# Dense feed-forward: most pairs of gate and up as seven block products of half size, each third pair as before

## The reference

```python
def swiglu(h, w_gate, w_up, w_down):
    return (jax.nn.silu(h @ w_gate) * (h @ w_up)) @ w_down
# layer 0, D_MODEL = 1024, D_FF = 2816
h = rmsnorm(x, norm_ffn[layer])
x = x + swiglu(h, ffn_w_gate[j], ffn_w_up[j], ffn_w_down[j])
```

## Time and profile before

| | |
|---|---|
| three runs | 1555.54, 1556.11, 1556.99 us; median 1556.11 |
| profiled execution, its own time | 1556.81 us, span 1555.1 us |
| TensorE busy | 1538.5 us, 99% of the span |
| VectorE, ScalarE, GpSimd busy | 65%, 54%, 15% |
| mean granted clock of TensorE | 0.997 of full |

### The profile page before, as it was taken

The page is one execution under the profiler, slowest core; times in us unless marked ns, Lnnn a source line. Parts: engine busy times, 40 slices in busy tenths (PEclk is TensorE's granted clock), DMA queues, the critical chain, the costliest instruction groups (busy, mean ns, idle before and its releaser), DMA issues.

```text
span 1555.1 us, 23275 instructions
## 1 busy us (share of the span) xinstructions
PE 1538.5 (99%) x7960; PEld 1309.2 (84%) x7961; DVE 1009.2 (65%) x1689; ACT 834.3 (54%) x1330; POOL 236.7 (15%) x290
## 2 busy tenths in 40 slices
PE   9999999999999999999999999999999999999997
PEld 6888888888888888888888888879898888889895
DVE  7657765755444443336557765776676988887587
ACT  6436665433223322324447664475576888886564
POOL 0204564000000000002015662010000011110000
PEclk9999999999999999999999999999999999999998
...
GB/s 228 196 99 69 74 55 82 95 136 136 156 138 138 95 91 98 99 91 155 102 92 69 72 55 90 195 57 320 257 256 254 358 385 372 388 384 266 240 255 134
DMA packets 89787, 265.71 MB, mean 171 GB/s; under 512 B 12497, under 2 KB 22737, under 8 KB 89680
## 3 DMA queue, kind: packets, MB, share of 16 engines
...
...
## 4 chain that ended last, share of the span: by engine, by line
PE 96%; DVE 2%; DMA 1%; issue 1%; ACT 0%; SPq 0%; DVEq 0%; ACTq 0%; POOLq 0%
PE ps L1698 19%; PE ps L1703 19%; PE ps L1699 19%; PE ps L2052 8%; PE ps L2027 5%; PE ps L2029 5%; PE ps L2028 5%; PE ps L2054 3%; PE ps L1865 2%; PE ps L1898 1%; PE ps L2026 1%; PE ps L2025 1%; PE ps L1878 1%; PE ps L1897 1%; PE ps L1877 1%; PE ps L2013 1%
## 5 line engine op out<-in xcount | busy, mean ns | idle before, releaser
L808 ACT ACTIVATE w_hi<-raw 128x1024 fp32r<-128x1024 f32 (+1 forms) x168 | 176.0, 1047 | 337.1 <-PE ps L1703 333.8
L1698 PE MATMUL ps<-h_hi,w_hi 128*128 128x512 f32 x880 | 350.6, 398 | 0.6 <-DVE k_lo L1245 0.4
L1699 PE MATMUL ps<-h_lo,w_hi 128*128 128x512 f32 x880 | 343.6, 390 | 0.0
L1703 PE MATMUL ps<-h_hi,w_lo 128*128 128x512 f32 x880 | 343.4, 390 | 0.0
L1157 DVE TENSOR_TENSOR w_lo<-raw,w_hi 128x1024 fp32r<-128x1024 f32 x136 | 164.3, 1208 | 124.1 <-ACT w_hi L808 123.9
L1162 DVE TENSOR_TENSOR m_lo<-m_raw,m_hi 128x1024 fp32r<-128x1024 f32 x144 | 167.9, 1192 | 61.1 <-ACT m_hi L851 60.3
L1703 PEld LDWEIGHTS ps<-h_hi,w_lo 128*128 128x128 f32 x880 | 165.2, 188 | 35.4
L1698 PEld LDWEIGHTS ps<-h_hi,w_hi 128*128 128x128 f32 x880 | 165.6, 188 | 27.0 <-DVE k_lo L1245 0.8
L1699 PEld LDWEIGHTS ps<-h_lo,w_hi 128*128 128x128 f32 x880 | 166.0, 189 | 25.9 <-issue 0.7
L851 ACT ACTIVATE m_hi<-m_raw 128x1024 fp32r<-128x1024 f32 x144 | 145.4, 1031 | 53.0 <-PE ps L2026 25.9
L2052 PE MATMUL ps<-xt,m_hi 128*128 128x320 f32 x592 | 154.3, 347 | 0.3 <-issue 0.3
...
...
...
## 6 DMA issues: line engine op xcount, KB each, us to landing
...
```

The costliest lines, as they stand in the source:

```text
L808: A.activation(split_of(n, 0, cols)[0], raw[:, n % RAW, 0:cols], ACT.Copy).then_inc(hi_ready, 1)
L1698: E.matmul(ps[:, bank, :], wh, hi, start=first, stop=False)
L1699: E.matmul(ps[:, bank, :], wh, lo, start=False, stop=False)
L1703: return E.matmul(ps[:, bank, :], wl, hi, start=False, stop=final)
```

## The change

A gate tile and an up tile, each cut into two halves of the 1024 inputs, are a 2 by 2 block matrix; the input cut into two halves of features and two of tokens is another. Their product is eight block products, each of 4 tiles of inputs by 256 tokens, or seven, if sums and differences of blocks are multiplied (Winograd's form). Pairs 3, 4, 6, 7, 9, 10, 12, 13, 15, 16, 18 and 19 are now made with seven, the other ten (0, 1, 2, 5, 8, 11, 14, 17, 20, 21) with two units as before. A product is 12 matmuls of 256 columns.

The tables of the order are these. A job is a product (`seven`) or a unit; `w_hi` and `w_lo` are now four slots of half a unit, and `FREED_BY` tells which jobs can be split when job `x` is done. Of a pair's products 0, 4 and 5 take weights as they are, 1, 2, 3 and 6 take sums:

```diff
+SEVENS = [f for f in range(PLAIN, KF - 2) if (f - PLAIN) % 3 < 2]
+JOBS = [job for f in range(KF) for job in
+        ([("seven", f, j) for j in range(7)] if f in SEVENS else [("unit", f, j) for j in range(2)])]
...
+def frees(x):
+    last = SLOT[x] + (1 if JOBS[x][0] == "unit" else 0)
+    return max(y for y in range(x) if SLOT[y] <= last - 4)
+FREED_BY = {d: [x for x in range(2, len(JOBS)) if frees(x) == d] for d in range(len(JOBS))}
...
+def on_pool(x):
+    return JOBS[x][0] == "seven" and JOBS[x][2] == 5
...
+def seven_weights(f, j):
+    gate, up = FFN_START + 2 * f, FFN_START + 2 * f + 1
+    low, high = slice(0, T), slice(T, UNIT)
+    return ((gate, low), (None, 1), (None, 2), (None, 0), (gate, high), (up, high), (None, 2))[j]
```

A buffer of `raw` is refilled when all products of its pair have been split (SyncE):

```diff
-if n >= RAW:
-    sp.wait_ge(lo_ready, n - RAW + 1)
+m = n - RAW
+if FFN_START + 2 <= m < FFN_END:
+    f, j = (m - FFN_START) // 2, m % 2
+    if f in SEVENS:
+        sp.wait_ge(seven_lo, low_by(f))
+        sp.wait_ge(seven_lo_pool, SEVENS.index(f) + 1)
+    else:
+        sp.wait_ge(seven_lo, LOW_COUNT[JOB[("unit", f, j)]])
+elif n >= RAW:
+    sp.wait_ge(lo_ready, m + 1)
```

GpSimd forms the sums of weights, four for a pair, in three tiles (`norm`, `y_other`, `y_sum`), the low part of product 5, and two of the four sums of tokens:

```diff
+    pool.tensor_tensor(sums[0][:], up[:, 0:T], up[:, T:UNIT], ALU.add).then_inc(sums_ready, 1)
+    pool.wait_ge(sums_ready, 4 * q + 1)
+    pool.tensor_tensor(sums[1][:], sums[0][:], gate[:, 0:T], ALU.subtract).then_inc(sums_ready, 1)
...
+    pool.tensor_tensor(sums[2][:], gate[:, 0:T], up[:, 0:T], ALU.subtract).then_inc(sums_ready, 1)
+if part == 2:
+    pool.wait_ge(sums_ready, 4 * q + 2)
+    pool.wait_ge(seven_lo, split(q, 2))
+    pool.tensor_tensor(sums[2][:], gate[:, T:UNIT], sums[1][:], ALU.subtract).then_inc(sums_ready, 1)
...
+x = JOB[("seven", SEVENS[q], 5)]
+pool.wait_ge(seven_hi, x - 1)
+hi, lo = job_split(x)
+pool.tensor_tensor(lo, job_full(x), hi.bitcast(F32), ALU.subtract).then_inc(seven_lo_pool, 1)
...
+if layer == 0:
+    pool.wait_ge(h32_ready, KD)
+    pool.wait_ge(t_full_ready, 2)
+    pool.tensor_tensor(t_full(2), h_block(0, second_half), h_block(0, first_half), ALU.subtract).then_inc(t_full_ready, 1)
+    pool.tensor_tensor(t_full(3), h_block(1, first_half), t_full(0), ALU.subtract).then_inc(t_full_ready, 1)
+    for part in range(3):
+        weight_sums(0, part)
+    for q in range(1, len(SEVENS)):
+        if q % 2:
+            weight_sums(q, 0)
+            low_on_pool(q - 1)
+        else:
+            low_on_pool(q - 1)
+            weight_sums(q, 0)
+        weight_sums(q, 1)
+        weight_sums(q, 2)
+    low_on_pool(len(SEVENS) - 1)
```

ScalarE first writes the normalised input in full precision (`h_full`, 8 tiles), then follows the jobs. Behind the second of two such pairs it does both silus and both high parts:

```diff
-split_hi(FFN_START + 2)
-for u in range(N_GU):
-    n = FFN_START + u
...
-    if u:
-        split_hi(n + 2)
...
+for k in range(KD):
+    A.activation(h_full(k), xs[:, k, :], ACT.Copy, scale=gains[:, gain_of(1), k:k + 1]).then_inc(h32_ready, 1)
+for x, (kind, f, j) in enumerate(JOBS):
+    if x < 2:
+        A.wait_ge(unit_done, FFN_START + x + 1)
+    else:
+        A.wait_ge(seven_done, x - 1)
+    if kind == "seven" and j == 0:
+        A.activation(quarters[:, 4 * f, :], seven_bank(f, 0), ACT.Copy).then_inc(p1_kept, 1)
+    for y in FREED_BY[x]:
+        job_high(y)
+    if x >= len(JOBS) - 2:
+        first_down(FFN_END + x - len(JOBS) + 2)
+    if kind == "seven" and j == 6 and f + 1 not in SEVENS:
+        silu(f - 1)
+        silu(f)
+        act_hi(f - 1)
+        act_hi(f)
+    if kind == "unit" and j == 0:
+        silu(f)
+    if kind == "unit" and j == 1:
+        act_hi(f)
+    if f in (1, 2):
+        token_parts_hi((2 * f + j - 2,))
+    if f and j == 0:
+        A.sem_inc(hi_ready, 2)
```

VectorE forms the other two sums of tokens, the low parts, the sums of products (one operation behind products 1, 3, 5 and 6), and behind the second pair the work that remains of both, which falls beside the units of the next pair:

```diff
-split_lo(FFN_START + 2)
...
+def gate_scaled_in_place(f):
+    V.tensor_tensor(silu_of(f), silu_of(f), rms_inv[:], ALU.mult).then_inc(ffn_scaled, 1)
...
+    if kind == "unit" and j == 0:
+        scaled(silu_of(f), pair_banks(f)[0]).then_inc(ffn_scaled, 1)
+    if x == 0:
+        V.wait_ge(h32_ready, KD)
+        V.tensor_tensor(t_full(1), h_block(1, second_half), h_block(0, second_half), ALU.subtract).then_inc(t_full_ready, 1)
+        V.wait_ge(t_full_ready, 1)
+        V.tensor_tensor(t_full(0), t_full(1), h_block(0, first_half), ALU.add).then_inc(t_full_ready, 1)
...
+    if kind == "seven" and j == 1:
+        V.wait_ge(p1_kept, q + 1)
+        if q % 2:
+            V.wait_ge(seven_sums, 4 * q)
+        V.tensor_tensor(quarters[:, 4 * f + 2, :], quarters[:, 4 * f, :], banks[:, 2, :], ALU.add).then_inc(seven_sums, 1)
+    if kind == "seven" and j == 3:
+        V.wait_ge(seven_sums, 4 * q + 1)
+        V.tensor_tensor(quarters[:, 4 * f + 1:u3_at(f) + 1:u3_at(f) - 4 * f - 1, :], twice(quarters[:, 4 * f + 2, :]),
+                        banks[:, 4:7:2, :], ALU.add).then_inc(seven_sums, 1)
+    if kind == "seven" and j == 5:
...
+    if kind == "seven" and j == 6:
+        V.tensor_tensor(quarters[:, 4 * f:4 * f + 2, :], quarters[:, 4 * f:4 * f + 2, :], banks[:, 1:8:6, :], ALU.add).then_inc(seven_sums, 1)
+    for y in FREED_BY[x]:
+        if not on_pool(y):
+            job_low(y)
...
+    if kind == "seven" and j == 6 and f + 1 not in SEVENS:
+        V.wait_ge(seven_sums, 4 * (q + 1))
+        gate_scaled_in_place(f - 1)
+        gate_scaled_in_place(f)
+        gated_up(f - 1, act_of(f - 1))
+        gated_up(f, act_of(f))
+        act_lo(f - 1)
+        act_lo(f)
+    if kind == "unit" and j == 1:
+        gated_up(f, ps[:, pair_banks(f)[1], :])
+        act_lo(f)
+    if f in (1, 2):
+        token_parts_lo((2 * f + j - 2,))
+    if f and j == 0:
+        V.sem_inc(lo_ready, 2)
```

up is no longer multiplied by `rms_inv`; instead each result of down is (`scaled`, ahead of the addition):

```diff
 V.wait_ge(unit_done, n + 1)
+scaled(ps[:, m % 2, :], m % 2).then_inc(ffn_scaled, 1)
+V.wait_ge(ffn_scaled, KF + m + 1)
 V.tensor_tensor(xs[:, m, :], xs[:, m, :], ps[:, m % 2, :], ALU.add).then_inc(x_updated, 1)
```

TensorE runs the jobs in order; `seven_tokens` gives a product its tile of `h_hi` or a sum of tokens (`t_low`, `t_top`, `a_both`):

```diff
-for u in range(2, N_GU):
-    f = u // 2
-    if f >= 2:
-        E.wait_ge(ffn_scaled if u % 2 == 0 else up_scaled, f - 1)
-    x_unit(FFN_START + u, UNIT_BANKS[u % 4])
...
+    wh, wl = job_split(x)
+    E.wait_ge(seven_hi, x - 1)
+    for k in range(4):
+        at = slice(k * P, (k + 1) * P)
+        hi, lo = seven_tokens(j, k)
+        E.matmul(out, wh[:, at], hi, start=k == 0, stop=False)
+        E.matmul(out, wh[:, at], lo, start=False, stop=False)
+        if k == 0 and on_pool(x):
+            E.wait_ge(seven_lo_pool, q + 1)
+        elif k == 0:
+            E.wait_ge(seven_lo, LOW_COUNT[x])
+        mm = E.matmul(out, wl[:, at], hi, start=False, stop=k == 3)
+    mm.then_inc(seven_done, 1)
```

More of the change, by code:

```diff
@@ L47 @@
 STEPS = 2 * HEADS * TT
+PLAIN = 3
+FFN_END = FFN_START + N_GU
+HALF_T = T // 2
 PT_BLOCKS = 10
```

209 lines of the change are left out of this document (177 added, 32 removed).

## The result

The changed kernel takes **1563.73 us** (median of 6 runs, 1561.49 to 1566.29) against 1556.39 us of the kernel before on the same chip (6 runs, 1555.54 to 1558.40). The ratio is **1.0045, 95% interval 1.0032 to 1.0058**: slower, by 7.3 us. The profiled execution took 1566.29 us, span 1564.5 us, 2.6 us more than the median.

What follows compares the result with a forecast made beforehand. TensorE was taken to bound the kernel, busy 1538.5 of 1555.1 us. The terms -9.6 + 3.7 + 0.7 + 3.9 + 8.0 = +6.7 us gave 1562.8 from the median of 1556.1; own range 1559.5 to 1568.

Steps and rivals of the forecast that it cites:

- the clock: Rival: TensorE's clock falls after its start waits; none expected, else up to 5.3 us, 1568; 0.10 shared with another case.
- What the seven products save: Twelve pairs as 84 matmuls of 256 columns, 10.08 us each instead of 10.88: 9.6 us saved.
- The start: Stage start: eight copies and two token sums delay unit 2's low part, so TensorE waits: +3.7 us.
- The end: Stage end: scaling the last of eight down results enters the chain before TensorE's next matmul: +0.7 us.
- The first group A: First pair of seven overall: product 4's low part late through token-sum parts taking turns with GpSimd: +3.9 us.
- The later groups A: Five later first pairs of seven after a pair of eight: VectorE and GpSimd alternate, 1.6 us each, +8.0 us.
- A4's low part: VectorE's weight remainder for product 4, first pair of seven: ends at 7.1 us, needed at 5.6, 1.5 late.
- U's late block: Pair of eight: VectorE and GpSimd work in turns ends 0.4 us late, counted within the 1.5 to 1.9.
- Group B: Second pair of seven after a pair of eight: slack everywhere, no wait, low parts ready before needed.
- rival of free engines: VectorE and GpSimd run at once without holding each other; -4.8 us, 1551.3, faster; chance 0.22.
- short exclusion: Rival: an engine holds the other out only while reading, 0.3 to 0.4 us less each; 1556.8; chance 0.18.
- The reading of the earlier trace: VectorE's low parts, with two SBUF inputs, and GpSimd's operations exclude each other for whole instructions, as probs<-probs,stat does.

Runs made afterwards that it cites:

- e_warm: The changed kernel with 5, 8 and 13 matmuls on zeros put where TensorE waits, no wait removed; 1559.11 us, ratio 1.0018.
- e_order2: The changed kernel with product 4's weight parts made before rounding the preceding activation, and GpSimd's product 5 low part between the next pair's first sums; 1554.16 us.
- e_start: The changed kernel with unit 2's parts made before the eight copies and token sums, and unit 3's low part before those sums; 1563.85 us, ratio 1.0048.
- e_narrow: The changed kernel with GpSimd's weight sums, product-6 sum and product 5 low part cut to 64 of 512 columns; stage 237.0 us, total 3314.21 not comparable.
- e_halves: The changed kernel with GpSimd's two first sums for every second pair of a group made in two halves of 256 columns; 1571.16 us, ratio 1.0091.

## Why the prediction was right, and where it was not

The forecast was 1562.8, the time 1563.7, and the sign, the places and the mechanism are as forecast. But the sum came out by two errors that cancel: the steps that I had summed were over-sized by 3.7 us in all (+6.7 for +3.0), and the clock, which I gave nothing, cost about 4.6 (1563.7 less e_warm's 1559.1; the two intervals leave some 2.5 us either way, and the trace has 3.0 + 1.45). That the number came out is luck. The sum of my steps with their measured sizes, -10.0 + 3.6 + 3.3 + 5.6 + 0.5, gives 1559.4, and that is what e_warm took (1559.1).

- **What the seven products save.** -9.6 forecast from four matmuls of attention; -10.0 measured (e_order2). Right; 256 columns cost 0.1197 each, not 0.120.
- **The start.** +3.7 forecast, +3.6 measured: the third matmul at 356.45 forecast, at 356.86 in an execution whose unit 0 starts 0.5 later. The eight copies, the two sums and the low part are in the order and of the length that I used. What I left out is what comes behind: the next low part stands beside GpSimd's token sum (3.02 us, has 1.16). It cost nothing here since unit 2 was late by more; e_start shows its price.
- **The end.** +0.7 forecast, +0.46 measured. The scaling puts 0.73 us into the chain (it starts at 710.54, the addition at 711.27), but the chain starts 0.27 earlier against TensorE: 2.52 us behind the first matmul of layer 1 (708.02), where the addition of the earlier trace rows stood 2.79 behind it (700.49).
- **The first group A.** +3.9 forecast (its own ends, 9.4 against 5.6, give 3.8), +3.3 measured. The turns are there as forecast: three low parts of 512 columns took 5.06 us together beside GpSimd, from 384.73.
- **The later groups A.** +8.0 forecast, +5.6 measured, 1.12 and not 1.6 each: this term was mis-sized. By my turns A4's low part ended 7.1 us after ScalarE saw the end of U1 and was needed at 5.6. In the trace it ended at 6.7 and was needed at 5.8 (ScalarE starts its next high part at 449.30, right behind U1; the low part ends at 456.03, the third matmul would have started at 455.06). Of the 0.2 by which it was needed later, 0.1 is a slip of mine: the third matmul of a product starts 0.24 us behind the first, and I had put 0.12. The turns are shorter than I reckoned: a low part ends 0.55 behind GpSimd's instruction and not 0.60, a sum 1.16 behind VectorE's and not 1.29. That the engine that is held does part of its work meanwhile would fit, but isn't shown. And the 0.4 us at which I had put U's late block doesn't exist; TensorE waits neither in U nor at A0.
- **Group B** has no wait, as forecast.
- **The rival of free engines** is refuted by the rows at 452 to 456 and by e_narrow, the **short exclusion** by the same rows: what is held ends 0.55 and 1.16 us behind the other, 0.13 less than its own length, where that rival had 0.3 to 0.4; e_halves shows that the hold goes by the other's instruction. The reading of the earlier trace rows, by which a low part behaves like probs<-probs,stat, was right, and the Trainium skill (SBUF — State Buffer, section "Who interferes with whom"), which says that this kind of instruction contends with GpSimd's and that the hold is exclusive, was right with it: L1374 went from 0.68 to 1.78, L1651 with its one SBUF input stayed at 0.67 to 0.69.
- **The clock.** This is the step that failed. I wrote that none was expected, because the clock had been full through the stage of the kernel before; but there TensorE never stood still in that stage, so those rows say nothing on a wait of 2 us. The nearest rows were behind the last matmul, 0.72, and they pointed the other way. The size that I gave for a whole unit, up to 5.3, was a little high (24 matmuls of 0.427 for 0.2267 are 4.8), but of the right order for what came, 3.0 + 1.45.
